# Expert stage of a hybrid block: each scatter-add split into two of 64 quarter rows, the second held for the running block's gate and up products

## The chip, the cores and the metric

The kernel runs on one core of a Trainium2 chip. A core has five engines with instruction streams of their own: TensorE (PE in the profile, with its weight loads as PEld), VectorE (DVE), ScalarE (ACT), GpSimd (POOL) and SyncE (SP, which here issues the weight transfers). They meet through semaphores. Sixteen DMA engines move data between the memory on the chip (SBUF) and HBM. The metric is the time of one execution in microseconds (us), as the median over several runs.

## The reference, cut to what matters

The program is one layer: attention and a recurrence side by side, an output projection, and then a mixture of experts, which is the only part that this change touches. Each of 2048 tokens picks one of 4 groups and in it 2 of 8 experts. An expert is three matrices, and its output goes back to the token's row, weighted by a gate:

```python
def expert_block(args):
    xb, e = args
    return (jax.nn.silu(xb @ w_g[e]) * (xb @ w_u[e])) @ w_d[e]
...
y = jnp.sum(out[slot_dest].reshape(n_tok, TOP_K, D) * gates[..., None].astype(h.dtype), axis=1)
```

The width D is 1024, an expert's inner width is 512, there are 32 experts, and all is float32. The result of the stage is x plus y.

## The kernel before, in words

The stage before this one has written x (with the mixing output added) into `out` and the normalized tokens into `h2` in HBM, and has sorted the 4096 (token, expert) pairs into blocks of `ROWS` = 32 tokens of one expert. With this input there are 144 blocks.

`run_experts` computes a block at a time. A token's row of 1024 numbers is treated as four quarter rows of 256, so that 32 tokens fill 128 partitions. For each block b, with j = b % 2 the number of its buffer:

- POOL gathers the 128 quarter rows of the block from `h2` into `xg[j]` by an indirect DMA (L2303); the row numbers stand in `take[j]`.
- DVE turns `xg[j]` into `xT` (L2412). There is one `xT`, so this waits for the gate and up products of the block before (`gu_done`).
- PE does the gate and up products, 64 matmuls into `gu_ps` (L2343, function `gate_up`), when `h_ready` says that `xT` is filled and that `gu_ps` of the block before has been read.
- ACT takes silu of the gate half (`sil`, L2397), DVE multiplies it with the gate weight and the up half (`h`, L2426) and turns the product (`hT`, L2430).
- PE does the down product, 32 matmuls into `y_ps` (L2352, function `down`). PE's order is gate_up(0), gate_up(1), down(0), gate_up(2), down(1), and so on: one block's down product stands behind the next block's gate and up products.
- ACT copies `y_ps` to `y[j]` (L2391), and POOL adds the 128 quarter rows of `y[j]` to the rows of `out` by an indirect DMA with an add (L2311); the row numbers stand in `put[j]`, which DVE fills (`number_rows`, L2417).

Two buffers each of `xg`, `take`, `y`, `put` and `gate` exist. `stored[j]` counts landed adds: ACT waits for it before it copies over `y[j]`, DVE before it writes over `put[j]`. `gathered[j]` counts landed gathers, and DVE waits for it before it turns `xg[j]`. POOL's order in the loop is, for block b: wait until `h` of block b+1 is done, gather block b+4's rows into the buffer that has just been turned, wait for `put` and `y` of block b, add block b. After the loop come the adds of the last two blocks, and waits for all that was stored.

SP refills one of three weight slots (`SLOTS` = 3, 6 MB each) whenever an expert's last down product is done. PE and the others walk the blocks in hardware loops, one nest over experts on PE and a loop over pairs of blocks on the others.

The counters start above zero: `h_ready` has got one increment and `rows_known` two before block 0, and `y_copied` starts with a credit of 16. So `h_ready >= b + 3` means that `h` of block b+1 is done, `rows_known >= b + 3` that `put` of block b is filled, and `gu_done >= b + 3` that the gate and up products of block b+2 are done.

Of the kernel before, what the change touches and what calls it, by code (L numbers as in the profile page):

```python
# [18 lines left out]
I32 = mybir.dt.int32  # L19
U32 = mybir.dt.uint32  # L20
ALU = mybir.AluOpType
# [3 lines left out]
P = 128  # L25
# [2093 lines left out]
def place_slots(nc, program, E_all, ranks, gates, totals, places, n_blocks, first_block, n_pairs, from_all, to_all, gate_all):  # L2119
# [6 lines left out]
    with ExitStack() as ctx:  # L2126
        sb, pb, sem = makers(nc, ctx, program)
        QUARTERS = [slice(q * ROWS, (q + 1) * ROWS) for q in range(4)]
        SHIFT = ROWS.bit_length() - 1
# [98 lines left out]
def run_experts(nc, program, n_blocks, first_block, n_pairs, from_all, to_all, gate_all, experts, h2_dram, out):  # L2228
# [9 lines left out]
    with ExitStack() as ctx:  # L2238
        sb, pb, sem = makers(nc, ctx, program)
        FT = FF // P  # L2240
        WARM = 5
        QUARTERS = [slice(q * ROWS, (q + 1) * ROWS) for q in range(4)]
        w_gu, w_d = experts.gate_up, experts.down
        gu_loaded, d_loaded = experts.gu_loaded, experts.d_loaded
        take = [sb(f"take7{j}", [P, 1], I32) for j in range(2)]
        put = [sb(f"put7{j}", [P, 1], I32) for j in range(2)]
        gate = [sb(f"gate7{j}", [P, 1]) for j in range(2)]
        xg = [sb(f"xg{j}", [P, D // 4]) for j in range(2)]
        xT = sb("xT", [P, KT * ROWS])
# [3 lines left out]
        y = [sb(f"y7{j}", [P, D // 4]) for j in range(2)]  # L2253
# [3 lines left out]
        rows_known, h_ready, gu_done, silu_ready, hT_ready, y_done, y_copied = [sem(f"p7_{n}") for n in names]  # L2257
        gathered = [sem(f"p7_gathered{j}") for j in range(2)]
        stored = [sem(f"p7_stored{j}") for j in range(2)]
        on_pe, on_pool = program.gates_passed  # L2260
        h2_quarters = h2_dram.rearrange("t (q d) -> (t q) d", q=4)
        out_quarters = out.rearrange("t (q d) -> (t q) d", q=4)
# [10 lines left out]
        def last_pair(eng):  # L2273
            return eng.value_load(n_pairs[0:1, 1:2], min_val=NE - 1, max_val=MAX_BLOCKS // 2 - 1)
# [10 lines left out]
        with nc.Block() as block:  # L2285
# [14 lines left out]
            @block.gpsimd  # L2300
            def _(pool):
                def gather(j):
                    pool.indirect_dma_start(out=xg[j][:, :], out_offset=None, in_=h2_quarters[:, :],  # L2303
                                            in_offset=bass.IndirectOffsetOnAxis(ap=take[j][:, 0:1], axis=0)).then_inc(gathered[j], 16)

                def add(b, j):
                    pool.wait_ge(rows_known, b + 3)
                    pool.sem_inc(on_pool, 1)
                    pool.wait_ge(y_copied, b + CREDIT + 1)
                    pool.sem_inc(on_pool, 1)  # L2310
                    pool.indirect_dma_start(out=out_quarters[:, :], out_offset=bass.IndirectOffsetOnAxis(ap=put[j][:, 0:1], axis=0),  # L2311
                                            in_=y[j][:, :], in_offset=None, compute_op=ALU.add).then_inc(stored[j], 16)

                def one_block(b, j, i, first):
                    pool.wait_ge(h_ready, b + 3)
                    pool.sem_inc(on_pool, 1)
                    gather(j)
                    add(b, j)

                pool.wait_ge(rows_known, 2)  # L2320
                for j in range(2):
                    gather(j)
                for j in range(2):
                    pool.wait_ge(h_ready, j + 1)
                    gather(j)
                last = last_pair(pool)
                pairs_of_blocks(pool, last, one_block)
                for j in range(2):
                    add(last * 2 + j, j)
                for j in range(2):  # L2330
                    pool.wait_ge(gathered[j], last * 16 + 32)  # L2331
                    pool.sem_inc(on_pool, 1)  # L2332
                    pool.wait_ge(stored[j], last * 16 + 16)  # L2333
                    pool.sem_inc(on_pool, 1)
                pool.drain()

# [48 lines left out]
            @block.scalar  # L2385
            def _(act):
                def copy_y(b, j, i):
                    act.wait_ge(y_done, b + 1)
                    if not isinstance(i, int) or i > 0:
                        act.wait_ge(stored[j], i * 16)  # L2390
                    act.copy(y[j][:, :], y_ps[:, 0:256]).then_inc(y_copied, 1)  # L2391

                def one_block(b, j, i, first):
                    if j == 0:
                        act.activation(warm[:, :], gate_all[:, 0:1], ACT.Silu)
                    act.wait_ge(gu_done, b + 1)
                    act.activation(sil[:, :], gu_ps[:, 0:P], ACT.Silu).then_inc(silu_ready, 1)  # L2397
                    if not first:
                        copy_y(b - 1, 1 - j, i - 1 + j)

                pairs_of_blocks(act, pairs_of(act), one_block)
                last = last_pair(act)
                copy_y(last * 2 + 1, 1, last)

            @block.vector
            def _(dve):
                def next_rows(j, b):
                    return dve.tensor_copy(take[j][:, :], from_all[:, bass.ds(b, 1)])

                def turn_rows(j, i):  # L2410
                    dve.wait_ge(gathered[j], i * 16 + 16)
                    dve.transpose(xT[:, :].rearrange("p (k t) -> p k t", k=KT), xg[j][:, :].rearrange("t (p k) -> t k p", k=KT))  # L2412

                def number_rows(b, j, i):
                    if not isinstance(i, int) or i > 0:
                        dve.wait_ge(stored[j], i * 16)
                    dve.tensor_copy(put[j][:, :], to_all[:, bass.ds(b, 1)]).then_inc(rows_known, 1)  # L2417

                def one_block(b, j, i, first):
                    dve.tensor_copy(gate[j][:, :], gate_all[:, bass.ds(b, 1)])  # L2420
                    dve.drain()
                    dve.wait_ge(gu_done, b + 1)
                    turn_rows(1 - j, i + j)
                    next_rows(1 - j, b + 3)
                    dve.wait_ge(silu_ready, b + 1)
                    dve.scalar_tensor_tensor(h[:, :], sil[:, :], gate[j][:, :], gu_ps[:, P:2 * P], ALU.mult, ALU.mult).then_inc(h_ready, 1)  # L2426
                    dve.drain()  # L2427
                    if not first:
                        dve.wait_ge(y_done, b)
                    dve.transpose(hT[:, :].rearrange("p (k t) -> p k t", k=FT), h[:, :].rearrange("t (p k) -> t k p", k=FT)).then_inc(hT_ready, 1)  # L2430
                    if not first:
                        number_rows(b - 1, 1 - j, i - 1 + j)

                for j in range(2):
                    next_rows(j, j).then_inc(rows_known, 1)
                turn_rows(0, 0)
                next_rows(0, 2).then_inc(h_ready, 1)
                pairs_of_blocks(dve, pairs_of(dve), one_block)
                last = last_pair(dve)
                number_rows(last * 2 + 1, 1, last)  # L2440


# [60 lines left out]
```

## Time and profile before

| | |
|---|---|
| median of 3 runs | 2784.62 us (2781.67 to 2787.75) |
| span of the profiled execution, first to last instruction | 2769.6 us |
| median less the profiled span | 15.0 us |
| PE busy in the span | 2604.3 us (94%) |
| first gate/up product of the expert stage | at 1928.1 us |
| last add issued | at 2760.0 us |
| adds (L2311) | 144, 1577 ns mean on POOL |
| gathers (L2303) | 146, 991 ns mean on POOL |

The profiled execution has no time of its own beside its span; the 15.0 us are what the runs have over it. Times in the rows count from the span's start. "Busy" of POOL for an indirect DMA is the time in which POOL prepares it, not the time of the transfer. "Idle before, releaser" names what an engine's idle time before an instruction ended with.

### The profile page before, as it was taken

Reading aid. Unit: us, or ns where it says so; the run is one execution under the profiler, and the core shown is the slowest. Engines: PE = TensorE matmul, PEld = TensorE weight load, DVE = VectorE, ACT = ScalarE, POOL = GpSimd, SP = SyncE. Lnnn points to the kernel's source line nnn. Section 1 sums busy time; section 2 is a strip of 40 time slices with the busy share of each in tenths; the row PEclk is TensorE's granted clock in tenths of the full one; section 3 lists DMA queues with packets and bytes.
Section 4 is the critical chain, followed back from the end, with each engine's and each line's share of the span. In section 5 each row is a group of like instructions: output and inputs, shape, how many; then the busy total and the mean of one; then the engine's idle time right before and its main releaser. Section 6 shows DMA issues by size and latency. Waiting matters only on the chain. (4 is left out here: it accounts for less than half of the span.)

```text
span 2769.6 us, 87168 instructions
## 1 busy us (share of the span) xinstructions
PE 2604.3 (94%) x37008; PEld 1718.1 (62%) x37009; DVE 1176.3 (42%) x2440; ACT 904.4 (33%) x1687; POOL 805.8 (29%) x916
## 2 busy tenths in 40 slices
PE   8999999999999998788888889996999999999998
PEld 3444444444477776677777745554776777777775
DVE  2333321212499998576666623335222222222222
ACT  1111110000377777666666533442111111111111
POOL 0000040000000000766666411112444444444444
PEclk9999999999999999899999999997999999999999
DMA  4111141111212221111112036531998997989893
GB/s 141 57 57 57 57 126 46 68 45 68 77 34 78 74 72 49 31 49 47 39 49 58 15 117 212 194 118 60 298 298 260 306 297 248 298 261 340 282 300 60
DMA packets 241149, 370.01 MB, mean 134 GB/s; under 512 B 35009, under 2 KB 134849, under 8 KB 238242
## 3 DMA queue, kind: packets, MB, share of 16 engines
q1 hardware_dynamic: 213186, 328.72, 34.6%
q0 software_dynamic: 27744, 38.03, 6.6%
q8 instruction: 179, 2.93, 0.4%
q14 instruction: 40, 0.33, 0.0%
HBM read 296.17 MB, written 70.52 MB: 132 GB/s over the span
## 5 line engine op out<-in xcount | busy, mean ns | idle before, releaser
L2343 PE MATMUL gu_ps<-gate_up_,xT 128*32 128x256 f32 x6336 | 425.0, 381 | 9.0 <-DVE h L2426 1.0
L2343 PEld LDWEIGHTS gu_ps<-gate_up_,xT 128*32 128x32 f32 x6336 | 274.1, 109 | 127.2 <-issue 65.4
L347 PE MATMUL ps<-low,high 128*128 128x512 f32 x768 | 337.6, 596 | 2.4 <-issue 2.4
L2412 DVE STREAM_TRANSPOSE xT<-xg 128x256 f32<-128x256 f32 x145 | 94.8, 654 | 517.0 <-PE gu_ps L2343 513.5
L2352 PE MATMUL y_ps<-down_,hT 128*32 128x256 f32 x4608 | 313.6, 379 | 0.6 <-ACT y L2391 0.6
L2303 POOL DMA_INDIRECT xg<-h,take x146 | 144.7, 991 | 425.0 <-DVE h L2426 403.3
L2352 PEld LDWEIGHTS y_ps<-down_,hT 128*32 128x32 f32 x4608 | 225.4, 110 | 46.2 <-ACT y L2391 1.1
L347 PEld LDWEIGHTS ps<-low,high 128*128 128x128 f32 x768 | 144.6, 192 | 173.4 <-issue 173.4
L2311 POOL DMA_INDIRECT out<-y,put x144 | 227.0, 1577 | 60.1 <-issue 55.2
L722 DVE TENSOR_TENSOR_SCAN h_all<-h_all 128x512 f32<-128x512 f32 x192 | 239.0, 1304 | 2.8 <-ACT h_all L680 2.3
L1782 PE MATMUL ps<-high 128*128 128x512 f32 x512 | 231.7, 603 | 7.1 <-DMA high<-mixT 7.1
L2397 ACT ACTIVATE sil<-gu_ps 128x128 f32<-128x128 f32 x144 | 40.1, 279 | 512.6 <-PE gu_ps L2343 512.6
L2343 PE MATMUL gu_ps<-high,xT 128*32 128x256 f32 x2880 | 199.0, 381 | 3.7
L447 PE MATMUL ps<-h_all,w_first 128*128 128x512 f32 x448 | 193.6, 592 | 0.0
L1782 PEld LDWEIGHTS ps<-high 128*128 128x128 f32 x512 | 95.3, 192 | 114.0 <-issue 113.2
L447 PE MATMUL ps<-h_all,low 128*128 128x512 f32 x384 | 165.8, 592 | 0.0
L2343 PEld LDWEIGHTS gu_ps<-high,xT 128*32 128x32 f32 x2880 | 129.5, 109 | 53.9 <-issue 29.9
L501 DVE TENSOR_TENSOR low<-low 128x2048 f32<-128x2048 f32 x13 | 29.8, 2293 | 296.8 <-ACT low L473 296.8
L447 PEld LDWEIGHTS ps<-h_all,w_first 128*128 128x128 f32 x448 | 85.0, 190 | 106.7 <-issue 106.7
L680 ACT ACTIVATE h_all<-ps 128x1024 f32<-128x1024 f32 (+3 forms) x160 | 144.2, 902 | 2.8 <-PE ps L625 2.7
L701 POOL TENSOR_TENSOR h_all<-h_all 128x2048 f32<-128x2048 f32 x2 | 10.4, 5193 | 441.9 <-DMA v_last<-v 441.9
L473 ACT COPY low<-ps 128x512 f32<-128x512 f32 x52 | 30.6, 588 | 319.2 <-PE ps L447 319.2
(326 smaller groups left out, 4319.0 us busy)
## 6 DMA issues: line engine op xcount, KB each, us to landing
down_<-in_w_exp_down SPq DMA_DIRECT2D x128, 512.0 KB
gate_up_<-in_w_exp_gate SPq DMA_DIRECT2D x88, 512.0 KB
gate_up_<-in_w_exp_up SPq DMA_DIRECT2D x88, 512.0 KB
high<-in_w_exp_gate SPq DMA_DIRECT2D x40, 512.0 KB
high<-in_w_exp_up SPq DMA_DIRECT2D x40, 512.0 KB
pT<-low SPq DMA_DIRECT2D x13, 1024.0 KB, 3.9
rkv<-pT SPq DMA_DIRECT2D x96, 128.0 KB, 2.5
high<-in_x SPq DMA_DIRECT2D x16, 512.0 KB, 4.0
```

Of the source, the lines that this page charges most:

```text
L347: done = pe.matmul(qkv_ps[:, part, :], hT[:, s, k, :], w_sb[:, k, part * SBW:(part + 1) * SBW], start=(k == 0), stop=(k == KT - 1))
L447: last = pe.matmul(p_ps[:, s, g, :], w[s][:, k, :], h_all[:, k, g * GT:(g + 1) * GT], start=(k == 0), stop=(k == KT - 1))
L473: act.copy(p_raw[:, 1 + g * GT:1 + (g + 1) * GT], p_ps[:, s, g, :]).then_inc(copied, 1)
L680: act.activation(keep[:, n % KEPT, :, 0:w], z_ps[n % 2][:, :, 0:w], ACT.Sigmoid, scale=-SCALE).then_inc(kept, 1)
L722: scan = dve.tensor_tensor_scan(out, rows, rows, prod[:, (n - 1) % KEPT, h, 0:1], ALU.mult, ALU.bypass)
L1782: done = pe.matmul(self.ps[:, s, half, :], self.rows[:, s, k, :], self.w[:, k, half * 512:(half + 1) * 512], start=(k == 0), stop=(k == KT ...
L2303: pool.indirect_dma_start(out=xg[j][:, :], out_offset=None, in_=h2_quarters[:, :], in_offset=bass.IndirectOffsetOnAxis(ap=take[j][:, 0:1], ...
L2311: pool.indirect_dma_start(out=out_quarters[:, :], out_offset=bass.IndirectOffsetOnAxis(ap=put[j][:, 0:1], axis=0), in_=y[j][:, :], in_offs ...
L2343: last = pe.matmul(gu_ps[QUARTERS[q], 0:2 * P].rearrange("t (x f) -> t x f", x=2), xT[:, k * ROWS:(k + 1) * ROWS], w_gu[s][:, k, :, q * P: ...
L2352: last = pe.matmul(y_ps[QUARTERS[q], 0:256], hT[:, k * ROWS:(k + 1) * ROWS], w_d[s][:, k, q * 256:(q + 1) * 256], start=(k == 0), stop=(k ...
L2397: act.activation(sil[:, :], gu_ps[:, 0:P], ACT.Silu).then_inc(silu_ready, 1)
L2412: dve.transpose(xT[:, :].rearrange("p (k t) -> p k t", k=KT), xg[j][:, :].rearrange("t (p k) -> t k p", k=KT))
```

## The change

Each add becomes two indirect DMAs, over the partitions 0 to 63 and 64 to 127 of `y[j]`. [...] In the loop POOL issues the first half where the whole add was, then waits until the gate and up products of block b+2 are done, and issues the second half; only then does it go on to the next block's gather. In the last two blocks the halves follow each other without that wait. Each block now adds 32 instead of 16 to `stored[j]`, and the waits for it count so.

```diff
+        HALVES = [slice(0, P // 2), slice(P // 2, P)]
-        put = [sb(f"put7{j}", [P, 1], I32) for j in range(2)]
+        put = [sb(f"put7{j}", [P // 2, 2], I32) for j in range(2)]
...
-                def add(b, j):
+                def add_half(j, half):
+                    rows = HALVES[half]
+                    pool.indirect_dma_start(out=out_quarters[:, :], out_offset=bass.IndirectOffsetOnAxis(ap=put[j][:, half:half + 1], axis=0),
+                                            in_=y[j][rows, :], in_offset=None, compute_op=ALU.add).then_inc(stored[j], 16)
+
+                def add_first(b, j):
                     pool.wait_ge(rows_known, b + 3)
                     pool.sem_inc(on_pool, 1)
                     pool.wait_ge(y_copied, b + CREDIT + 1)
                     pool.sem_inc(on_pool, 1)
-                    pool.indirect_dma_start(out=out_quarters[:, :], out_offset=bass.IndirectOffsetOnAxis(ap=put[j][:, 0:1], axis=0),
-                                            in_=y[j][:, :], in_offset=None, compute_op=ALU.add).then_inc(stored[j], 16)
+                    add_half(j, 0)
 
                 def one_block(b, j, i, first):
                     pool.wait_ge(h_ready, b + 3)
                     pool.sem_inc(on_pool, 1)
                     gather(j)
-                    add(b, j)
+                    add_first(b, j)
+                    pool.wait_ge(gu_done, b + 3)
+                    pool.sem_inc(on_pool, 1)
+                    add_half(j, 1)
...
                 for j in range(2):
-                    add(last * 2 + j, j)
+                    add_first(last * 2 + j, j)
+                    add_half(j, 1)
...
-                    pool.wait_ge(stored[j], last * 16 + 16)
+                    pool.wait_ge(stored[j], last * 32 + 32)
...
-                        act.wait_ge(stored[j], i * 16)
+                        act.wait_ge(stored[j], i * 32)
...
-                        dve.wait_ge(stored[j], i * 16)
-                    dve.tensor_copy(put[j][:, :], to_all[:, bass.ds(b, 1)]).then_inc(rows_known, 1)
+                        dve.wait_ge(stored[j], i * 32)
+                    dve.tensor_copy(put[j][:, 0:1], to_all[HALVES[0], bass.ds(b, 1)])
+                    dve.tensor_copy(put[j][:, 1:2], to_all[HALVES[1], bass.ds(b, 1)]).then_inc(rows_known, 1)
```

## Rows read from the trace of the kernel before

**Rows 1.** Stage windows: length; busy PE, PEld, DVE, ACT, POOL; PEclk; DMA share; GB/s
```profile
1928.00:2704.30 776.30, 764.23 (x12908) 565.02 (x12911) 203.20 (x804) 96.77 (x335) 342.37 (x267) 1.00 0.88 288
2704.30:2755.00 50.70, 50.08 (x883) 36.95 (x877) 14.14 (x57) 6.59 (x23) 23.10 (x18) 1.00 0.29 49
```

**Rows 2.** Waits of PE and PEld, 1928 to 2762 us: total, times, longest
```profile
PE gu_ps L2343 <- DVE h L2426: 1.0, 1, 1.0
...
PEld gu_ps L2343 <- issue: 95.3, 217, 0.8
PEld gu_ps L2343 <- DVE h L2426: 2.3, 3, 1.5
```

**Rows 3.** One block in order of time: start us, us, what, idle before
```profile
2305.63 0.38 PE L2352 MATMUL y_ps<-down_,hT 128*32 128x256 f32 x1
...
2306.11 0.28 ACT L2397 ACTIVATE sil<-gu_ps 128x128 f32<-128x128 f32 x1 [3.59 <-PE gu_ps L2343]
...
2306.81 0.34 DVE L2426 SCALAR_TENSOR_TENSOR h<-sil,gate,gu_ps 128x128 f32<-128x128 f32 x1
2307.21 2.96 PEld L2343 LDWEIGHTS gu_ps<-high,xT 128*32 128x32 f32 x48
...
2307.91 0.37 ACT L2391 COPY y<-y_ps 128x256 f32<-128x256 f32 x1 [1.52 <-PE y_ps L2352]
2307.96 0.99 POOL L2303 DMA_INDIRECT xg<-h,take  x1 [2.83 <-DVE h L2426]
2308.18 0.11 DVE L2417 COPY put<-to_all 128x1 int32 x1
...
2309.29 1.58 POOL L2311 DMA_INDIRECT out<-y,put  x1 [0.34 <-issue]
...
2311.88 0.28 ACT L2397 ACTIVATE sil<-gu_ps 128x128 f32<-128x128 f32 x1 [3.45 <-PE gu_ps L2343]
```

**Rows 4.** The copy that waits for landed adds, all 144
```profile
L2391 ACT COPY y<-y_ps x144: 372/373/377, 1938.2 to 2758.9; 128x256 f32<-128x256 f32 x144
...
  PE y_ps L2352: 219.3, 144
```

**Rows 5.** DMA after the add issued at 2740.86, columns of Rows 1
```profile
2743.00:2743.50 0.50, 0.50 (x16) 0.43 (x12) 0.26 (x1) 0.28 (x1) 0.00 (x0) 1.00 1.17 106
...
2744.00:2744.50 0.50, 0.50 (x16) 0.42 (x10) 0.19 (x1) 0.00 (x0) 0.00 (x0) 1.00 0.15 21
```

**Rows 6.** DVE's small copies, ns min/median/max: take without, put with POOL's gather beside
```profile
L2408 DVE COPY take<-from_all x147: 99/110/153, 1921.0 to 2755.0; 128x1 int32 x140, 128x1 int32<-128x1 int32 x7
...
L2417 DVE COPY put<-to_all x144: 98/111/164, 1938.6 to 2757.2; 128x1 int32 x141, 128x1 int32<-128x1 int32 x3
```

**Rows 7.** The last two adds and what stands before them, in order of time
```profile
2754.28 0.28 ACT L2397 ACTIVATE sil<-gu_ps 128x128 f32<-128x128 f32 x1 [3.28 <-PE gu_ps L2343]
...
2757.44 1.56 POOL L2311 DMA_INDIRECT out<-y,put  x1 [3.86 <-DVE put L2417]
2758.86 0.37 ACT L2391 COPY y<-y_ps 128x256 f32<-128x256 f32 x1 [2.40 <-PE y_ps L2352]
2760.03 1.55 POOL L2311 DMA_INDIRECT out<-y,put  x1 [1.03 <-ACT y L2391]
```

**Rows 8.** Two blocks of 5.74 us, with much and little DMA, columns of Rows 1
```profile
2100.36:2106.10 5.74, 5.67 (x103) 4.33 (x99) 1.57 (x6) 0.80 (x3) 2.57 (x2) 1.00 1.07 378
2112.02:2117.76 5.74, 5.74 (x105) 4.02 (x109) 1.56 (x7) 0.80 (x4) 2.58 (x3) 1.00 0.29 47
```

**Rows 9.** y copies that end those two blocks, in order of time
```profile
2100.44 0.37 ACT L2391 COPY y<-y_ps 128x256 f32<-128x256 f32 x1 [1.52 <-PE y_ps L2352]
...
2106.18 0.37 ACT L2391 COPY y<-y_ps 128x256 f32<-128x256 f32 x1 [1.53 <-PE y_ps L2352]
...
2111.96 0.37 ACT L2391 COPY y<-y_ps 128x256 f32<-128x256 f32 x1 [1.52 <-PE y_ps L2352]
...
2117.70 0.37 ACT L2391 COPY y<-y_ps 128x256 f32<-128x256 f32 x1 [1.52 <-PE y_ps L2352]
```

## Prediction

> **What bounds the kernel now.** I read the page first (PE busy 94% of a span of 2769.6 us), then the windows over the expert stage. From 1928.0 to 2755.0 us TensorE is busy 764.23 + 50.08 = 814.31 of 827.0 us, 98.5%, at the granted clock 1.00 (the 2.4 GHz level), while GpSimd is busy 365.47 us, VectorE 217.34 and ScalarE 103.36 [rows 1]. The DMA share is high, 0.88, until the weights are all loaded, and 0.29 after that. So three things could be the bound: PE, the transfers, or the loop through POOL.
>
> The waits say which [rows 2]. In the whole stage PE's matmuls waited once for `h`, 1.0 us. Its weight loads waited 2.3 us for `h` in three places and 95.3 us for "issue", which is no other engine. No row has PE waiting for a weight load, for `xT` behind a gather, or for an add. The reader should see that an add has no direct reader on PE at all: it frees `y` and `put`, and these hold up ScalarE and VectorE before they could hold up PE.
>
> The timeline of one block gives the places [rows 3]. I call T the start of `sil`, 2306.11, which is when the gate and up products are seen to be done; the next T is 2311.88, a period of 5.77 us. Against T: `h` ends at +1.04 (2306.81 + 0.34), PE's first weight load of the next block starts at +1.10, `y` is copied from +1.80 to +2.17, the gather runs on POOL from +1.85 to +2.84, `put` is written at +2.07, the add runs on POOL from +3.18 to +4.76. POOL is then idle until +5.77 + 1.85. It is busy 2.57 of 5.77 us. The narrow place is the 0.06 us between the end of `h` and PE's weight load: PE's next block hangs directly on VectorE's chain in the first 1.04 us after T. Nothing else is near the path.
>
> **The change part by part.** The sum stands against the profiled execution, span 2769.6 us; the runs shown have 15.0 us more by their median, which lies outside the span, and I carry it over unchanged.
>
> *POOL's preparation.* The trace has only indirect DMAs of 128 rows: 0.99 us for a gather, 1.58 us for an add [rows 3]. A half add costs x between 0.79 us (half of 1.58, all of it by the row) and 1.58 us (all of it fixed). I take 1.18, the middle, since the only other row, the gather's 0.99, lies near it. From the semaphore to the start POOL needs 0.8 us: `h` ends 2307.15, the gather starts 2307.96. Between two DMAs it needs 0.34 us [rows 3].
>
> *The held half.* It starts at T + 0.8 (the hold binds: the first half, issued in the block before, is through well ahead of T), ends at +1.98. Behind it on POOL stands the gather, which moves from +1.85 to +2.32 (+2.72 at x = 1.58) and behind that the next first half, from +3.18 to +3.65, ending at +4.83. The next held half is due at 5.77 + 0.8 = +6.57, so POOL has 1.7 us to spare, 0.9 us at x = 1.58; it becomes the bound only for x over 2.05 us ((6.57 - 0.8 - 0.34 - 0.99 - 0.34) / 2). Cost in the loop: 0.
>
> *Who waits for the gather.* It fills a buffer that is turned two blocks later, at T + 11.54, against an issue at +1.85: 9.7 us, in which gathers have landed so far, since PE shows no stall behind `xT` and `h` [rows 2]. Now 9.2 us are left, at the worst 8.8. Cost 0 if gathers land in that, and a delay on the path if they need between 8.8 and 9.7 us. The nearest landing that the rows show is that of an add, below, at under 3.7 us.
>
> *Who waits for the held half.* The copy of `y` and VectorE's `put` two blocks on need both halves landed. Before: add at +3.18, copy at 1.80 + 11.54 = +13.34, so 10.2 us of time, and in all 144 copies ScalarE waited for PE alone [rows 4]. So an add lands in under 10.2 us also among the weight loads. From below: the add issued at 2740.86, with no weights beside it, moves its data between 2743.0 and shortly after 2744.0 [rows 5], so it lands after about 3.4 us. Now: the held half is issued at 5.77 + 0.8 = +6.57 and the copy is due at +13.34, which leaves 6.8 us. Landing after 3.4 to 6.8 us costs nothing; later than that the copy of `y` slips. PE asks for that copy only when its next down product starts: in rows 3 a copy ends at 2308.28 and the down product before it had started at 2305.63, so the next one comes at 2311.40, 3.1 us later. The point from which it costs is therefore 6.8 + 3.1 = 9.9 us. I take 0, and keep (10.2 - 9.9) = 0.3 us a block as the upper end.
>
> *VectorE.* 144 more copies of [64 x 1], each by the row of `put` 0.11 us [rows 6], after `hT` at about T + 2.2, where the engine is idle for the next 3.6 us. Its wait for landed adds stands in the same idle time. Cost 0; without this cover it would be 144 x 0.11 = 16 us.
>
> *ScalarE and PE* get no instruction. The bytes of the transfers are the same, the number of transfers grows by 144.
>
> *The end.* Here nothing covers. Now [rows 7]: T of the last block 2754.28; last but one add 2757.44; last copy of `y` ends 2759.23; last add 2760.03 to 2761.58. With x = 1.18: held half of the block before these two 2755.08 to 2756.26; halves of the last but one block 2757.44 to 2758.62 and 2758.96 to 2760.14; of the last block 2760.48 to 2761.66 and 2762.00 to 2763.18. That is 1.6 us later. The last transfer has half the data: the whole one took some 1.3 us for its data [rows 5], so about 0.65 us come back. Net +0.95. At x = 0.79 the same steps give 2761.95, +0.37 - 0.65 = -0.3; at x = 1.58 they give 2764.78, +3.2 - 0.65 = +2.55.
>
> **Sum**: 2769.6 + 0.95 = 2770.55, and with the 15.0 us outside, 2785.6 us.
>
> *A rule against the change.* The row says that a whole add lands 3.4 us after POOL starts it, wherever its 128 KB go [rows 5]. The Trainium skill, "DMA: Bandwidth & Descriptors", Rules for kernel authors, says that two transfers to disjoint halves of the partitions don't pay, since they run on the same DMA engines one after the other, and its section on the anatomy of one DMA puts a fixed 2.0 us on each. Estimated by that page alone, the last two halves would take 2 x (2.0 + 0.15) us where one whole takes 2.3, which makes the end 2.0 us later in place of 0.95; no row here can show a half's cost.
>
> **The rivals.**
> (A) *The held half lands too late.* For it: 3.4 us of time are taken away and the DMA share is 0.88 in this part of the stage [rows 1]. Against it: it needs over 9.9 us, where a whole add needs under 10.2. The place is ScalarE's copy of `y` behind `stored`, then PE's down product behind `y_copied`. Price up to 0.3 us in each of the some 135 blocks beside weight loads: +40 us, 2826.
> (B) *VectorE's narrow place is hit.* POOL was idle from T to T + 1.85; now it prepares the held half from T + 0.8, while `h` runs from +0.70 to +1.04. This is the rival on the other side that I take most seriously, since `h` is 0.06 us ahead of PE. Every 0.1 us beyond that costs 142 x 0.1 = 14 us, 2800. Against it: `put` is copied inside the gather's time on POOL and takes 98/111/164 ns, `take` is copied with POOL idle and takes 99/110/153 [rows 6]; and `h` had begun before POOL starts. The Trainium skill, "SBUF — State Buffer", Who interferes with whom, says that VectorE and GpSimd share a pair of ports as an exclusive lock, the later one blocking fully. By that rule `put` should have taken up to the 0.9 us that the gather had left; the rows disagree for a copy this small, and for `h` they are silent.
> (C) *Smaller bursts help PE.* Without weight loads the stage has 883 matmuls in 50.7 us, 57.4 ns each, and with them 12908 in 776.3 us, 60.1 ns [rows 1]: 2.7 ns x 96 = 0.26 us a block. If halving the add's burst took all of it away it would be 135 x 0.26 = -35 us, 2751. Against it: a block with DMA share 1.07 and one with 0.29 (the weights pausing) both take 5.74 us from copy to copy [rows 8, 9], so it isn't the traffic that makes the difference.
> (D) *The hold never holds*, because the first half is through only after the next products are done. It would need x near 2 us; the halves would follow each other, and the time be the same 2785.6 us as long as POOL keeps up.
>
> **How the numbers follow.** About 0.2% (5.6 us) is what a measurement of this kernel can tell from no change; the three runs of before span 6.1 us. Forecast: 0.81, of which I give 0.76 to a time within 0.2%, 0.02 to faster and 0.03 to slower by chance and by the end's upper bound. A: 0.05. B: 0.09. C: 0.03. D: 0.02, the same time. So faster 0.05, same 0.78, slower 0.17. The range, 2780 to 2796, holds the forecast with the runs' own spread of 3 us on either side and the end's bounds (-0.3 to +2.55), and goes up into B as far as 0.07 us more a block; A, C and the rest of B lie outside.
>
> **What would show it.** Each step right: PE's period stays 5.7 to 5.8 us; POOL has three DMAs a block, the held half 0.8 us after `sil` starts, each half add near 1.18 us; `h` still takes 0.34 us; ScalarE's copy still waits for PE alone, or now and then some tenths for a landing without PE noticing; the last half ends near 2763.2 when counted from the same start. Wrong: `h` or the weight load behind it later against T (B), a wait of PE for `y` (A), a period of 5.5 us in mid-stage (C). The forecast as a whole falls if the expert stage, first product to last, changes by over 3 us.

## The result and the profile after

| | median, us | runs |
|---|---|---|
| kernel before, in the same session | 2783.57 | 4 (2781.67 to 2787.75) |
| changed kernel | 2803.72 | 4 (2802.67 to 2806.86) |

The ratio is 1.007, 95% interval 1.0055 to 1.0084: slower by some 20 us, where 2785.6 us was forecast. The experiments below add a second half to this result: there are sessions (one chip, kernels run side by side) in which the kernel before takes about 2780 us and sessions in which it takes about 2700 us (2780-us and 2700-us sessions from here on). In the one session of the second kind in which the changed kernel ran beside the kernel before, the two could not be told apart (ratio 1.0009, 0.9997 to 1.0022).

The stage between 2000 and 2600 us, in the columns of [rows 1], first of the kernel after, then of a second profile of the kernel before (2790.33 us in its own run):

```profile
2000.00:2600.00 600.00, 583.56 (x9625) 449.95 (x9620) 171.89 (x704) 72.81 (x252) 385.86 (x302) 1.00 0.87 281
```

```profile
2000.00:2600.00 600.00, 588.28 (x9867) 439.34 (x9861) 155.34 (x615) 74.12 (x256) 264.02 (x206) 1.00 0.88 285
```

In the same 600 us PE does 9625 matmuls after and 9867 before: 62.3 and 60.8 ns for one. At 96 a block that is 0.15 us a block, and some 20 us over the stage: most of the loss is spread over the blocks, and it is in PE's pace. PE's busy time hardly shows it (583.56 and 588.28 of 600). The first profile of the kernel before, of a quicker execution, has 9979 matmuls in this window, so the size of the loss is less sure than its place: from the first gate/up product to the last copy of `y` the changed kernel takes 859.3 us, and the two profiles of the kernel before 830.8 and 840.0.

The waits of PE's weight loads in the stage of the kernel after, beside [rows 2] (total us, times, longest):

```profile
PEld gu_ps L2352 <- issue: 114.6, 252, 0.9
PEld y_ps L2361 <- issue: 15.0, 28, 0.6
```

"Issue" (idle time that ended with nothing the profile can name) has grown from 95.3 to 129.6 us (107.9 in the second profile of before), and no other engine has come in: the waits for `h` and `y` are 5.1 and 1.5 us. One block of the kernel after, in order of time, beside [rows 3]; T is 2331.49:

```profile
2331.49 0.28 ACT L2406 ACTIVATE sil<-gu_ps 128x128 f32<-128x128 f32 x1 [3.31 <-PE gu_ps L2352]
2332.20 0.34 DVE L2436 SCALAR_TENSOR_TENSOR h<-sil,gate,gu_ps 128x128 f32<-128x128 f32 x1
2332.25 1.41 POOL L2309 DMA_INDIRECT out<-y,put  x1 [1.46 <-PE gu_ps L2352]
...
2332.86 2.75 PEld L2352 LDWEIGHTS gu_ps<-gate_up_,xT 128*32 128x32 f32 x54 [0.17 <-issue]
2333.96 1.01 POOL L2304 DMA_INDIRECT xg<-h,take  x1 [0.30 <-issue]
2335.27 1.43 POOL L2309 DMA_INDIRECT out<-y,put  x1 [0.30 <-issue]
2336.01 0.16 PEld L2352 LDWEIGHTS gu_ps<-gate_up_,xT 128*32 128x32 f32 x5 [0.40 <-issue]
2336.76 0.17 PEld L2352 LDWEIGHTS gu_ps<-gate_up_,xT 128*32 128x32 f32 x5 [0.59 <-issue]
2336.87 1.79 PEld L2361 LDWEIGHTS y_ps<-down_,hT 128*32 128x32 f32 x32
2337.45 0.28 ACT L2406 ACTIVATE sil<-gu_ps 128x128 f32<-128x128 f32 x1 [3.22 <-PE gu_ps L2352]
```

The reader should see two gaps of PE's weight loads, 0.40 and 0.59 us, while the last preparation of POOL (2335.27 to 2336.70) runs, and a period of 5.96 us. The kernel before had such gaps too, and I had not shown them. In the block of [rows 3] they are these, and the add on POOL runs from 2309.29 to 2310.87:

```profile
2307.21 2.96 PEld L2343 LDWEIGHTS gu_ps<-high,xT 128*32 128x32 f32 x48
2310.72 0.63 PEld L2343 LDWEIGHTS gu_ps<-high,xT 128*32 128x32 f32 x16 [0.55 <-issue]
```

A half takes 1.41 us on POOL, against 1.58 for the whole. The end of the kernel after, beside [rows 7]; T of the last block is 2785.73:

```profile
2786.49 1.40 POOL L2309 DMA_INDIRECT out<-y,put  x1 [1.23 <-PE gu_ps L2352]
2789.43 1.41 POOL L2309 DMA_INDIRECT out<-y,put  x1 [1.53 <-DVE put L2427]
2791.14 1.41 POOL L2309 DMA_INDIRECT out<-y,put  x1 [0.30 <-issue]
2792.85 1.41 POOL L2309 DMA_INDIRECT out<-y,put  x1 [0.30 <-issue]
2794.57 1.41 POOL L2309 DMA_INDIRECT out<-y,put  x1 [0.30 <-issue]
```

Behind the last add POOL waits for what was stored and then drains (the last line of POOL's program). This is the drain, first of the kernel before, then of the kernel after:

```profile
L2335 POOLq DRAIN  x1: 5452/5452/5452, 2763.9 to 2763.9; - x1
```

```profile
L2344 POOLq DRAIN  x1: 7045/7045/7045, 2797.7 to 2797.7; - x1
```

From the last T to the end of the span it is 15.3 us before (2769.6 less 2754.28) and 19.4 us after (2805.1 less 2785.73). So 4.0 us, about a fifth of the loss, lie behind the loop.

### The profile page after: what moved, and what is told of

The parts are those of the page before. It is cut to its first block and busy times, and to the rows that moved or that the text cites. A ratio compares the mean times of both kernels' runs of the same rounds, so it can differ in the third digit from the quotient of the medians.

```text
span 2805.1 us, 87809 instructions
## 1 busy us (share of the span) xinstructions
PE 2616.7 (93%) x37008; PEld 1747.6 (62%) x37009; DVE 1204.8 (43%) x2584; ACT 904.0 (32%) x1687; POOL 988.5 (35%) x1060
## 5 line engine op out<-in xcount | busy, mean ns | idle before, releaser
L2309 POOL DMA_INDIRECT out<-y,put x288 | 408.6, 1419 | 257.8 <-PE gu_ps L2352 199.3
L2352 PE MATMUL gu_ps<-gate_up_,xT 128*32 128x256 f32 x6336 | 432.6, 380 | 16.0 <-issue 5.2
L2352 PEld LDWEIGHTS gu_ps<-gate_up_,xT 128*32 128x32 f32 x6336 | 285.3, 110 | 132.3 <-issue 79.8
L2352 PEld LDWEIGHTS gu_ps<-high,xT 128*32 128x32 f32 x2880 | 141.3, 110 | 46.7 <-issue 34.8
L2400 ACT COPY y<-y_ps 128x256 f32<-128x256 f32 x144 | 53.7, 373 | 275.1 <-PE y_ps L2361 266.2
```

Of the source, the lines that this page charges most:

```text
L2352: last = pe.matmul(gu_ps[QUARTERS[q], 0:2 * P].rearrange("t (x f) -> t x f", x=2), xT[:, k * ROWS:(k + 1) * ROWS], w_gu[s][:, k, :, q * P: ...
```

## The experiments

Theories are named as in the expectations. S: PE gets its instructions later while POOL prepares indirect DMAs, and the amount of preparation decides what that costs. W: POOL's preparation of indirect DMAs slows the supply of instructions to PE, and where it lies in the block decides what that costs. H: the held half's place beside VectorE's chain. A: an add matters by its transfer. L: it comes with the loading of a program. J: it is a condition of the whole session.

### Session 1 (kernel before: 2786.63 us, 7 runs)

A second profile of the kernel before, unchanged.

> The kernel before, once more, for a second profile. Both theories: the stage from the first gate/up product to the last copy of y, which took 830.8 us in the first profile and 859.3 us after the change, comes out at 830 to 840 us, with the copy-to-copy period at a median of 5.75 us. If it comes out near 850, most of what the two first profiles differ by is not the change's.

Measured: 2790.33 us; first gate/up product to last copy of `y` 840.0 us, period 5.81 us. The first profile had been of a quick execution, and as a run's time is its span and 1.8 us (2790.33 and 2788.5 here), my "15.0 us outside the span" was mostly a difference between executions. Half of the 18.9 us between the two profiles lies ahead of the expert stage, which begins at 1928.1 us in the one and at 1937.8 us in the other.

Halves without the hold, a change to the changed kernel:

```diff
                     add_first(b, j)
-                    pool.wait_ge(gu_done, b + 3)
-                    pool.sem_inc(on_pool, 1)
                     add_half(j, 1)
```

> The changed kernel without the hold: both halves of an add follow each other. Theory S (PE gets its instructions later while POOL prepares indirect DMAs, so PE's stall in the gate/up products grows with POOL's preparation time, 2.57 us a block before, 3.85 after): the same time as the changed kernel, ratio to before 1.007, with PE's longest gap between weight loads again ending near the end of POOL's last preparation of the block. Rival H (it is the place of the held half, at 0.8 us after the products are done, beside VectorE's chain): ratio 1.000, since nothing of POOL is there now.

Measured: 2889.85 us, ratio 1.0359 (1.0338 to 1.038). Both theories named too small a number. A block of it:

```profile
2334.51 1.43 POOL L2309 DMA_INDIRECT out<-y,put  x1 [0.40 <-issue]
2335.19 0.16 PEld L2350 LDWEIGHTS gu_ps<-gate_up_,xT 128*32 128x32 f32 x4 [0.17 <-issue]
2335.93 0.37 PEld L2350 LDWEIGHTS gu_ps<-gate_up_,xT 128*32 128x32 f32 x10 [0.58 <-issue]
...
2336.25 1.41 POOL L2309 DMA_INDIRECT out<-y,put  x1 [0.30 <-issue]
...
2337.56 1.01 PEld L2359 LDWEIGHTS y_ps<-down_,hT 128*32 128x32 f32 x19 [0.57 <-issue]
2337.73 0.28 ACT L2404 ACTIVATE sil<-gu_ps 128x128 f32<-128x128 f32 x1 [4.33 <-PE gu_ps L2350]
```

There is one gap of 0.6 us in PE's loads beside each late preparation: the first in the gate and up products, the second now in the down product. The waits of the whole stage say the same: "issue" ahead of the down product's loads, of which the kernel before has none.

```profile
PEld gu_ps L2350 <- issue: 100.1, 225, 0.8
PEld y_ps L2359 <- issue: 90.7, 199, 0.6
```

A second, equal preparation costs a second, equal gap, and the period is 6.5 us.

The whole add held, not split, a change to the kernel before:

```diff
-                def add(b, j):
+                def add(b, j, hold=False):
...
                     pool.wait_ge(y_copied, b + CREDIT + 1)
                     pool.sem_inc(on_pool, 1)
+                    if hold:
+                        pool.wait_ge(gu_done, b + 3)
+                        pool.sem_inc(on_pool, 1)
...
-                    add(b, j)
+                    add(b, j, hold=True)
```

> The kernel before with the whole add held until the gate and up products of two blocks on are done, not split. Theory S: POOL's preparation is 2.57 us a block as before, so no time is lost by its amount; ratio 0.997 to 1.001, less than 1 if a preparation that ends earlier in the block lets PE catch up. Rival H: ratio 1.007, as in the changed kernel, since the add is prepared from 0.8 us after the products on.

Measured: 2704.51 us, ratio 0.9699 (0.9683 to 0.9715). H falls, and S by amount too: the preparation is 2.57 us a block as before, and 82 us are gone. The numbers of split (+103) and hold (-82) add up to 21, beside the 20 of the change. That is no proof of two separate parts, since here the whole add is held and in the change one half.

No adds at all (POOL raises their semaphore):

```diff
-                    pool.indirect_dma_start(out=out_quarters[:, :], ...
+                    pool.sem_inc(stored[j], 16)
```

> The kernel before without the 144 adds (their semaphore is raised by POOL itself, the expert results are left out of the output). Theory S: POOL prepares 0.99 us a block in place of 2.57, so by the change's own slope (0.2 us for 1.28 us) the period falls by 0.25 us to 5.5 us, ratio 0.987. Rival H: the adds had nothing to do with PE, ratio 0.999 to 1.000, period 5.75 us.

Measured: 2694.48 us, ratio 0.9669 (0.9653 to 0.9685), period 5.18 us; neither side had expected so low a time. Holding the add recovers in the stage what leaving it out does: from the first gate/up product to the last copy of `y` it is 757.4 us with the hold and 756.5 us without adds, and in both profiles the period is 5.18 us.

### Session 2 (kernel before: 2778.99 us, 13 runs)

Both halves held and issued together, the gather behind them:

```diff
                 def add_first(b, j):
...
-                    add_half(j, 0)
...
                     pool.wait_ge(gu_done, b + 3)
                     pool.sem_inc(on_pool, 1)
+                    add_half(j, 0)
                     add_half(j, 1)
...
                     add_first(last * 2 + j, j)
+                    add_half(j, 0)
                     add_half(j, 1)
```

> The changed kernel with both halves held: they are prepared from about 0.8 and 2.5 us after the products are done (T), and the gather behind them from about 4.2 to 5.2 us. Theory W (POOL's preparation of any indirect DMA takes instruction supply from PE, and it costs where it runs beyond about T + 3.7 us, when PE has used up what was dispatched ahead): the gather now lies in the bad stretch, period 5.5 to 5.7 us, ratio to before 0.98 to 1.0. Rival A (only an add matters, by its transfer or its semaphore, and holding it is what helps): period 5.2 us, ratio 0.97, as with the whole add held.

Measured: 2741.37 us, ratio 0.9869 (0.9847 to 0.9892), mean period 5.47 us. The ratio is in W's range and the period just below it, but the trace doesn't have W's reason:

```profile
2329.97 1.64 PEld L2362 LDWEIGHTS y_ps<-down_,hT 128*32 128x32 f32 x32
2332.51 3.18 PEld L2353 LDWEIGHTS gu_ps<-gate_up_,xT 128*32 128x32 f32 x64 [0.91 <-issue]
```

All 64 loads run without a gap although the gather is prepared late, at T + 4.2 us (T is 2331.06, the gather starts at 2335.28). The lost time lies ahead of the block's first load, beside the first held half. So in this block a gather does not do what an add does at that place, and W as I had stated it is too wide. In the whole stage it is the same: 42.0 us of "issue" ahead of the gate and up loads, 37 of them within 2.3 us of T, and 24.3 us of waiting for `h`. The late place is thus not the only one at which an add can cost: two adds on end cost at the start of the block.

POOL busy with arithmetic in the add's place:

```diff
-                    pool.indirect_dma_start(out=out_quarters[:, :], ...
+                    pool.drain()
+                    pool.tensor_tensor(made[:, :], work[:, :], work[:, :], ALU.mult).then_inc(stored[j], 16)
```

> The kernel before with each add replaced by a multiplication of 128 x 512 numbers on POOL at the same place, about 1.5 us long by the row of POOL's 128 x 256 (909 ns) and 128 x 2048 (5193 ns) operations; expert results are left out of the output. If it is the preparing of a DMA that PE suffers from (theory W as stated): period 5.2 us, ratio 0.967, as without adds. If any work on POOL at that place does it: period 5.75 us, ratio 1.00.

Measured: 2767.90 us, ratio 0.9958 (0.9948 to 0.9968), which neither side named: POOL itself came late here (501.7 us of "issue" before the multiplications, and VectorE then waited 278.8 us for gathers). In the 23 blocks in which the multiplication started 3.6 to 4.5 us after T, the median period was 5.18 us, and in the whole stage PE's gate and up loads have 14.5 us of "issue", against 107.9 with adds; what PE lost it lost waiting for `h` (92.5 us). That speaks for the DMA preparation, with a reserve: a multiplication took 1.04 us and not the 1.58 us of an add, and seldom stood in its place.

Only the first 64 quarter rows added, in the old place:

```diff
-                    pool.indirect_dma_start(out=out_quarters[:, :], out_offset=bass.IndirectOffsetOnAxis(ap=put[j][:, 0:1], axis=0),
-                                            in_=y[j][:, :], in_offset=None, compute_op=ALU.add).then_inc(stored[j], 16)
+                    pool.indirect_dma_start(out=out_quarters[:, :], out_offset=bass.IndirectOffsetOnAxis(ap=put[j][0:64, 0:1], axis=0),
+                                            in_=y[j][0:64, :], in_offset=None, compute_op=ALU.add).then_inc(stored[j], 16)
```

> The kernel before with only the first 64 quarter rows added, at the old place (the other 64 are left out). Theory W: preparation is 1.42 us in place of 1.58, and that is what counts, so the period is 5.65 us, a little under 5.75. Rival A, by the bytes: half the transfer, so half of the 0.57 us that an add costs, period 5.45 us.

Measured: 2782.76 us (one run), period 5.755 us, as with the whole add. Half the bytes and 0.14 us less preparation changed nothing. A falls (5.45 us), and W's 5.65 us was missed as well: no slope by duration shows in this range.

No indirect DMA in the loop at all (the adds replaced as in the run without adds, and `gather(j)` taken out of the loop too; the four gathers ahead of the loop stay, and VectorE waits for these alone):

> Neither adds nor, after the first four, gathers: POOL prepares nothing in the loop (the experts work on wrong rows and their results are left out). Theory W: PE already ran at its own rate with the gathers alone, so the period stays at 5.18 us; but PE's sequencer, which reached the down product 3.66 us after T with gathers and 4.72 us with adds as well, gets there earlier still, by some tenths of a us, if a gather's preparation also takes supply from it. Rival A: the gather has no part in it, so the sequencer is there at 3.66 us again.

Measured: 2693.25 us (one run), period 5.18 us, and PE's sequencer (which hands PE its instructions) is at the down product at T + 3.66 us, just as in the run without adds, which had the gathers. The gather alone takes nothing from PE here.

### Session 3 (kernel before: 2700.09 us, one run)

> The whole add held, but until h of two blocks on is done instead of its gate and up products: prepared from T + 1.85 to 3.4 us, the gather behind it from 3.8 to 4.8. Theory W (any preparation that runs in the last part of the gate/up products, beyond about T + 3.7, costs): the gather is now in that part, period 5.5 to 5.75 us and a time of 2750 to 2785 us. If only an add costs, or if what helped was that the add is no longer tied to the copy of y: period 5.2 us, 2705 us.

> The kernel before with each add replaced by a gather of 128 quarter rows into a tile that nobody reads (expert results are left out of the output): POOL prepares it from T + 3.18 to 4.17 us, 0.99 us in place of 1.58. Theory W: a gather does it too, but it ends 0.6 us earlier, so the period is between 5.18 (no second transfer) and 5.75 (the add), about 5.3, and PE's sequencer gets to the down product later than the 3.66 us without a second transfer. If it is the adding: period 5.18 us and 3.66 us.

> The changed kernel without its first halves (64 of the 128 quarter rows of each block are left out): the held half from T + 0.8 to 2.2 us, the gather from 2.5 to 3.5, nothing after it. Theory W: period 5.18 to 5.2 us, 2705 us or less, so that all that the changed kernel loses is lost by the first half, which the held half and the gather push to T + 3.8 to 5.2. If a third preparation or the held half's place costs by itself: over 5.3 us.

The edits were `wait_ge(h_ready, b + 4)` in place of the wait for `gu_done`; a gather from `h2` into a tile of its own in place of the add; and `add_half(j, 0)` taken out of the changed kernel, with the waits for `stored` back at 16 a block. One run each. Measured: 2710.97, 2701.20 and 2702.45 us, periods of 5.20, 5.18 and 5.18 us. None of them tells anything apart, because the kernel before was at 2700 us here as well: with the add at its old place and no stall. That put the whole reading in doubt: the quick runs of sessions 1 and 2 could have been luck.

### Session 4 (kernel before: 2701.98 us, 31 runs)

> The kernel before as a kernel of its own beside the kernel before. In three calls it took 2770 to 2790 us, in the last one 2700 us. Theory L (PE's stall comes or stays away with each loading of a program, whatever POOL does): the two copies can differ by 80 us. Theory W (POOL's late preparation causes it): both 2770 to 2790 us. Theory J (it is a condition of the whole call or chip, and in the good one there is no stall for any kernel): both alike, at 2700 or at 2780.

Measured: 2702.14 us, ratio 1.0003 (0.9991 to 1.0016). The two copies agree, here as in session 1, which speaks against L.

> The changed kernel once more. Theory W: 2804 us, 1.007 of the kernel before. Theory L: 2804 or about 2705 us, by chance. Theory J: 1.007 if the kernel before is at 2780, and near 1.00 if that is at 2700.

Measured: 2703.92 us, ratio 1.0009 (0.9997 to 1.0022).

> The halves without the hold once more, 2890 us last time. Theory W: 2890 us, 1.036. Theory L: 2890 or about 2705 us, by chance. Theory J: 1.036 if the kernel before is at 2780, near 1.00 if that is at 2700.

Measured: 2704.32 us, ratio 1.0015 (1.0002 to 1.0027), down from 2889.85.

> The hold without the split once more, 2704 us last time. Theory W: 2704 us, 0.970 of a kernel before at 2787. Theory L: 2704 or 2780 us, by chance. Theory J: 2704 us whatever the kernel before takes, if holding removes the stall; 1.00 where that is at 2700.

Measured: 2701.86 us, ratio 1.0003 (0.9993 to 1.0013). Theory J it is: in such a session no form of the add costs PE anything that shows in its pace. (The longer end of the changed kernel is there here too, 18.9 us from the last T to the end of the span against 15.1; it is too small for these runs to tell.) The stage of the unchanged kernel in session 4, and its "issue" waits:

```profile
2000.00:2600.00 600.00, 596.11 (x10976) 368.19 (x10972) 173.42 (x687) 82.83 (x287) 293.60 (x230) 1.00 0.96 316
```

```profile
PEld gu_ps L2343 <- issue: 18.9, 36, 0.9
```

10976 matmuls, 54.7 ns for one, with PE 99.4% busy, where [rows 1] has 60.1 ns with PE 98.4% busy. Nearly a tenth of PE's time was lost, and nearly all of it inside "busy".

### Sessions 5 to 7: the hold again

> The whole add held, not split, in another call. If the kernel before is at 2780 us there (the condition in which PE stalls), theory W and J say 2704 us, 0.970, with PE's sequencer at the down product about 4.0 us after T where the kernel before has 4.7; chance in the first call would show as 2780 us. If the kernel before is at 2700 us, the ratio is 1.00 and says nothing more.

> The whole add held once more. If the kernel before is at 2780 us in this call: 2704 us and 0.970 by theories W and J, 2780 us if the first result was chance. If the kernel before is at 2700 us: 1.00, nothing more.

> The whole add held, a last call. With the kernel before at 2780 us: 2704 us, 0.970 (W and J), or 2780 us (chance). With the kernel before at 2700 us: 1.00.

Measured: 2704.25 us beside 2705.84, ratio 0.9999 (0.999 to 1.0009); 2702.49 beside 2702.26, ratio 1.0002 (0.9988 to 1.0015); and in session 7, with the kernel before at 2782.07 us, 2702.17 us, ratio 0.971 (0.9694 to 0.9727). So the hold alone keeps PE at its pace in a session in which the kernel before loses it, a second time. Over the sessions, that of the result among them, the kernel before was at 2779 to 2787 us in four and at 2700 to 2706 us in four.

That session 7 was a 2780-us session for the held kernel too, and that the hold only keeps the disturbance from PE, is seen at the register operation with which PE's sequencer begins a down product (start, us). First the hold in session 7 and in session 4, each with the `sil` whose start is a T:

```profile
L2352 PEldq ALU_OP  x1: 36/36/36, 2333.2 to 2333.2; - x1
2334.40 0.28 ACT L2400 ACTIVATE sil<-gu_ps 128x128 f32<-128x128 f32 x1 [1.17 <-PE gu_ps L2346]
```

```profile
2332.12 0.28 ACT L2400 ACTIVATE sil<-gu_ps 128x128 f32<-128x128 f32 x1 [3.00 <-PE gu_ps L2346]
L2352 PEldq ALU_OP  x1: 36/36/36, 2335.8 to 2335.8; - x1
```

Then the unchanged kernel in session 4, with its `sil`, the unchanged kernel of [rows 3], and the changed kernel of the block above:

```profile
L2349 PEldq ALU_OP  x1: 36/36/36, 2332.9 to 2332.9; - x1
2334.43 0.28 ACT L2397 ACTIVATE sil<-gu_ps 128x128 f32<-128x128 f32 x1 [3.00 <-PE gu_ps L2343]
```

```profile
L2349 PEldq ALU_OP  x1: 36/36/36, 2310.8 to 2310.8; - x1
```

```profile
L2358 PEldq ALU_OP  x1: 32/32/32, 2336.8 to 2336.8; - x1
```

In session 7's hold and session 4's unchanged kernel the `sil` shown is the next one, and T is that less the period of 5.18 (2329.22 and 2329.25). Against their T the five stand at +4.0, +3.7, +3.7, +4.7 and +5.3 us; over all 144 blocks the medians are 4.03, 3.66, 3.66, 4.72 and 5.30 us. PE reaches the down product's loads 4.72 us after T at full pace. So the hold's own add delays the sequencer by 0.4 us in a 2780-us session and not at all in a 2700-us one, but the sequencer stays ahead of PE; with the add in its old place it is level with PE, and PE runs dry; with the change it is later still.

This also leaves little of L. By L it would have been chance that in the 2780-us sessions the kernels with a late add (the unchanged one, the changed one, the split, the one with half the rows) all lost pace and those without (the hold twice, no adds, no DMAs) all kept it.

## Why the prediction was wrong

**The step that failed** is the reading of the waits: "Its weight loads waited 2.3 us for `h` in three places and 95.3 us for 'issue', which is no other engine". I took 98.5% busy for a bound and set 95.3 us aside since nothing was named as its releaser. Most of those 95 us were a gap of some 0.55 us a block beside POOL's add, and 76 of them are gone in a 2700-us session (18.9 left; 17.4 and 16.5 with the hold in sessions 1 and 7). From that came "*ScalarE and PE* get no instruction" and "Cost in the loop: 0". The term was not small but absent: what a preparation on POOL costs PE. In 2780-us sessions it measured, by median periods, about 0.57 us a block for an add at its old place (5.75 less 5.18), another 0.75 for a second half behind a first (6.51 less the 5.76 of the run with half the rows), and 0.8 in the changed kernel (5.97 less 5.18). I put these 0.8 down to the first half, which the held half and the gather push from T + 3.2 to T + 3.8 us. That part is argued from the gaps: the run without the first half fell in a 2700-us session.

The Trainium skill, "Perfetto Trace Analysis", Identifying the Most-Contended Engine, warns that TensorE's matmul busy share is a bad measure of how near a kernel is to the limit. The rows here agree: 98.4 against 99.4% for nearly a tenth in pace. It advises two others in its place. One is the share of the weight loads, and that misleads here as well: 73% (439.34 of 600) in session 1, 61% (368.19) in the unchanged kernel of session 4. The other is the matmul work done per time in the window, and that is what told here, as the count of matmuls in 600 us (9867 and 10976).

**Rival C** named the right symptom ("57.4 ns each, and with them ... 60.1 ns") and a wrong cause, the traffic. That blocks with DMA share 1.07 and 0.29 took the same 5.74 us [rows 8] was chance, since they lost time in different places:

```profile
2103.25 0.39 PEld L2343 LDWEIGHTS gu_ps<-gate_up_,xT 128*32 128x32 f32 x11 [0.46 <-issue]
```

```profile
2112.00 3.36 PEld L2343 LDWEIGHTS gu_ps<-gate_up_,xT 128*32 128x32 f32 x63 [0.64 <-issue]
```

The first gap stands beside the add (on POOL from 2101.83 to 2103.41). The second stands ahead of the block's first load, with nothing on POOL; session 4 has gaps at that place too, in its 18.9 us of "issue". What speaks against the traffic is session 4: a matmul took 54.7 ns there at a DMA share of 0.96.

**Rival A** did not come about. In the changed kernel of the result ScalarE's copy waited for halves to land 6.7 us in 4 places, and in session 4 112.1 us in 58 places, and even there PE's down products waited only 0.6 us for a copy, as the working of that step has it:

```profile
ACT y L2400 <- DMA out<-y,put: 112.1, 58, 3.1
PE y_ps L2361 <- ACT y L2400: 0.6, 1, 0.6
```

**Rival B** did not either: `h` takes 0.34 us and starts 0.71 us after T at the median, before and after, with POOL's held half beside it. Its sign came true (a weight load later against T, +1.37 in the block above), without its mechanism: `h` ends at +1.05 as ever, and the loads ahead of that one are what ends late. The port rule that B takes from the Trainium skill ("SBUF — State Buffer", Who interferes with whom) was not tested by these rows: the section limits it to certain VectorE instructions (two-port modes, or two inputs in SBUF), and no row shows `put` or `h` to be one.

**The half's price**: x is 1.41 us, not 1.18, within the bounds of 0.79 and 1.58. POOL's places followed from it: held half at +0.76, gather at +2.47, first half at +3.78.

**The end** was the second term that was mis-sized. The last preparation ends 10.25 us after the last T (2795.98 less 2785.73), against 7.30 before [rows 7]: +2.95 us, where I had +1.6 and an upper bound of +3.2. POOL's wait for the last half ended 3.1 us after the half's start (2797.64), where that for the whole add took 3.8 (2763.80), so the smaller transfer did give back 0.7 us, and the last landing is 2.4 us later against T. What I had at nothing is the drain behind it: 7.05 us in place of 5.45, +1.6. Together +4.0 us, where I had +0.95.

**What stays open.** What makes a session one or the other is not known. It is not the chip alone (chip 10 had both), nor the program (the unchanged kernel had both), and the transfers look alike: counted from the traces' semaphore updates, an add of the unchanged kernel lands 7.0 us after its start at the median in session 1 and 7.1 us in session 4, and a packet of either kind takes as long. One thing does separate the traces. Each add raises its semaphore by 16, and in the 2700-us sessions the traces hold 93 to 100% of these updates, in the 2780-us ones 48 to 79%, also of the held kernel that keeps its pace (1776 of 2304 in session 7, 2156 in session 4). So in the 2780-us sessions the recording of events loses more of them. Whether that shares its cause with the stall, or has a part in it, no run here can tell.

How preparing an add takes instructions from PE is argued only from places and gaps. The Trainium skill, "Runtime: NRT & Kernel Launch", Instruction fetch mechanics, says that a jump out of the loaded pages makes the sequencer fetch by DMA and stalls it; a page load as the cause is not borne out here: the transfers of the changed kernel between 2020 and 2600 us have no instruction queue among them (the two rows are all there are), and in the split kernel without the hold it has two packets, where its stage has over 400 "issue" waits:

```profile
q1 hardware_dynamic: 60532, 138.40, 65.1%
q0 software_dynamic: 20113, 25.40, 22.2%
```

```profile
q8 instruction: 2, 0.03, 0.0%
```

Whether a late gather could do it in a 2780-us session was seen in one kernel only (both halves held), and the hold until `h`, the gather in the add's place and the held half alone were never run in one.

## What to carry to other kernels

Count matmuls per microsecond against the best stretch you know; a busy share near 100% says nothing of pace, and an "issue" wait that recurs in every block is a cost until shown otherwise. Where PE runs short instructions in a loop, try GpSimd's indirect adds right after PE's products of a block, and as few as can be: here the whole add held, so that it starts 0.8 us after them, without the split, is the best version, 0.970 and 0.971 of the kernel before in two sessions and equal to it in three. That "right after" is what helps is shown for a whole add in this kernel and no further. And time a kernel in more than one session before its trace is taken for the rule: the same program had two times 3% apart.

## What the runs showed of the hardware

- Preparing an indirect add of 64 rows takes GpSimd 1.41 us and one of 128 rows 1.58 us; a gather of 128 rows takes 0.99 us. The price is mostly per instruction, so splitting one costs nearly double.
- In some sessions each add prepared from about 3.2 us after a block's products on left a gap of 0.55 to 0.6 us in TensorE's weight loads; in others none did, with the same granted clock of 1.00 in the stage.
- GpSimd's drain at the end of the program took 5.45 us behind whole adds and 7.05 us behind halves, in sessions of either kind.
- TensorE's 128 x 256 matmuls on 32 columns ran at 54.7 ns each undisturbed, and were shown as 379 ns long at either pace.
